# Low parts of a kernel's weights made by ScalarE and an accumulating DMA instead of by VectorE

## What is computed

```python
u = rmsnorm(h, norm_g[l])
proj = jnp.einsum('bld,de->ble', u, w_in[l])
hq, hf, hi, hz, aq, ak, av, az, ga, gb = jnp.split(proj, offs, axis=-1)
oA = hgrn2_chunked(...)          # gated linear recurrence, per head
oB = ...                         # softmax attention of two components, per head
yA = jnp.einsum('blw,wd->bld', oA * jax.nn.silu(hz), w_branch_a[l])
yB = jnp.einsum('blw,wd->bld', oB * jax.nn.silu(az), w_branch_b[l])
m = jax.nn.sigmoid(ga) * yA + jax.nn.sigmoid(gb) * yB
h = h + jnp.einsum('bld,de->ble', m, w_out[l])
out = rmsnorm(h, final_g)
```

## Time and profile before

| | |
|---|---|
| profiled execution | 753.44 us (span 751.7 us) |
| median of three runs | 753.66 us |
| TensorE busy | 731.2 us, 97% of the span |
| VectorE busy | 453.1 us, 60% |
| ScalarE busy | 281.0 us, 37% |
| GpSimd busy | 23.0 us, 3% |
| VectorE's low parts (line 252) | 104 x 1222 ns = 127.1 us |
| ScalarE's high parts (line 247) | 104 x 1052 ns = 109.4 us |
| DMA | 63.44 MB, 27.8% of 16 engines' span |

### The profile page before, as it was taken

The page is one execution under the profiler, slowest core; times in us unless marked ns, Lnnn a source line. Parts: engine busy times, 40 slices in busy tenths (PEclk is TensorE's granted clock), DMA queues, the critical chain, the costliest instruction groups (busy, mean ns, idle before and its releaser), DMA issues.

```text
span 751.7 us, 12966 instructions
## 1 busy us (share of the span) xinstructions
PE 731.2 (97%) x4665; PEld 653.9 (87%) x4665; DVE 453.1 (60%) x1019; ACT 281.0 (37%) x548; POOL 23.0 (3%) x34
## 2 busy tenths in 40 slices
PE   2999999999999999999999999999999999999996
PEld 2998999999899899999989989998888888888885
DVE  4567569568667856956866785695643333233342
ACT  5414442642552444264155235425423222232232
POOL 2000000000000000000000000000000000000000
PEclk9899999999999999999999999999999999999999
DMA  7421220230122132023012213302323323323603
GB/s 265 122 76 57 86 84 12 72 112 28 56 87 81 50 90 84 2 82 112 28 56 84 84 35 104 85 1 85 112 85 112 95 87 98 112 84 98 237 29 113
DMA packets 105416, 63.44 MB, mean 84 GB/s; under 512 B 2066, under 2 KB 100772, under 8 KB 105396
## 3 DMA queue, kind: packets, MB, share of 16 engines
q1 hardware_dynamic: 105076, 62.52, 27.5%
q10 hardware_dynamic: 320, 0.66, 0.3%
HBM read 61.07 MB, written 2.10 MB: 84 GB/s over the span
## 4 chain that ended last, share of the span: by engine, by line
PE 96%; SPq 1%; issue 1%; DMA 1%; DVE 0%; ACT 0%; POOLq 0%; POOL 0%; DVEq 0%; ACTq 0%
PE ps L385 26%; PE ps L386 26%; PE ps L387 26%; PE ps L506 3%; PE ps L576 2%; PE ps L602 2%; PE ps L492 1%; PE ps L593 1%; PE ps L603 1%; PE ps L540 1%; PE ps L539 1%; PE ps L547 1%; PE ps L522 1%; DMA rows_in<-in_da_norm_g 1%; PE ps L531 1%
## 5 line engine op out<-in xcount | busy, mean ns | idle before, releaser
L385 PE MATMUL ps<-uT_hi,w_hi 128*128 128x512 f32 (+3 forms) x960 | 321.6, 335 | 0.0
L386 PE MATMUL ps<-uT_lo,w_hi 128*128 128x512 f32 (+3 forms) x960 | 308.7, 322 | 0.0
L387 PE MATMUL ps<-uT_hi,w_lo 128*128 128x512 f32 (+3 forms) x960 | 307.9, 321 | 0.0
L385 PEld LDWEIGHTS ps<-uT_hi,w_hi 128*128 128x128 f32 x960 | 181.6, 189 | 16.4 <-issue 3.2
L252 DVE TENSOR_TENSOR w_lo<-w_raw,w_hi 128x1024 fp32r<-128x1024 f32 x104 | 127.1, 1222 | 109.9 <-ACT w_hi L247 108.9
L387 PEld LDWEIGHTS ps<-uT_hi,w_lo 128*128 128x128 f32 x960 | 181.1, 189 | 13.9
L386 PEld LDWEIGHTS ps<-uT_lo,w_hi 128*128 128x128 f32 x960 | 181.6, 189 | 11.6
L247 ACT ACTIVATE w_hi<-w_raw 128x1024 fp32r<-128x1024 f32 x104 | 109.4, 1052 | 87.5 <-PE ps L387 84.3
L808 ACT ACTIVATE e<-e,small 128x144 f32<-128x144 f32 (+3 forms) x64 | 36.1, 565 | 41.9 <-DVE small L1200 41.9
L375 POOL TENSOR_TENSOR small<-small 128x4 f32<-128x4 f32 x16 | 16.1, 1008 | 507.3 <-DVE small L1135 362.7
L1133 DVE TENSOR_REDUCE small<-sq 128x4 f32<-128x512 f32 x16 | 11.0, 686 | 33.3 <-ACT sq L800 33.3
(11 more groups left out here) (185 smaller groups left out, 993.4 us busy)
## 6 DMA issues: line engine op xcount, KB each, us to landing
w_raw<-in_w_in SPq DMA_DIRECT2D x80, 512.0 KB, 3.7
w_raw<-in_w_branch_a SPq DMA_DIRECT2D x8, 512.0 KB, 3.6
w_raw<-in_w_branch_b SPq DMA_DIRECT2D x8, 512.0 KB, 3.6
w_raw<-in_w_out SPq DMA_DIRECT2D x8, 512.0 KB, 3.8
x_in<-in_x SPq DMA_DIRECT2D x4, 512.0 KB, 7.8
x_res<-in_x SPq DMA_DIRECT2D x4, 512.0 KB, 6.4
out<-y_out SPq DMA_DIRECT2D x8, 256.0 KB, 2.3
rope<-in_c_rope SPq DMA_DIRECT2D x1, 528.0 KB, 6.0
```

Source lines behind the costliest of these rows:

```text
L385: pe.matmul(dst, w[0], rhs[0], start=start, stop=False, skip_group_check=True)
L386: pe.matmul(dst, w[0], rhs[1], start=False, stop=False, skip_group_check=True)
L387: return pe.matmul(dst, w[1], rhs[0], start=False, stop=stop, skip_group_check=True)
```

## The change

Units 0 to 6 stay as they were. From unit 7 on (`BY_DMA` = 7) VectorE makes no low parts. ScalarE writes, right behind the high part, its negative into `w_lo` (`scale=-1.0` on the raw unit), and a DMA that GpSimd issues adds the raw unit to it in place. Two semaphores `low_added` count these DMAs, for even and odd ones. SP waits for them in `low_seen`, ahead of the load that reuses the place in `w_raw`, and counts up `lo_ready` for TensorE. GpSimd's order puts the adds of `conv(0)` and `conv(1)` ahead of a head's first power, those of `conv(2)` to `conv(6)` between the two powers and that of `conv(7)` behind the second.

```diff
@@ convert_hi @@
         act.activation(w_hi[:, slot, :], w_raw[:, slot % RAW, :], ACT.Copy).then_inc(hi_ready, 1)
+        if not isinstance(u, int) or u >= BY_DMA:
+            act.activation(w_lo[:, slot, :], w_raw[:, slot % RAW, :], ACT.Copy, scale=-1.0).then_inc(neg_ready, 1)
+    def add_raw(pool, p, u, slot):
+        pool.wait_ge(neg_ready, u - BY_DMA + 1)
+        pool.sem_inc(adds_begun, 1)
+        pool.dma_start(w_lo[:, slot, :], w_raw[:, slot % RAW, :], accum_op=ALU.add).then_inc(low_added[p % 2], 16)
@@ sync @@
+            def low_seen(h, u):
+                if h is None and u < BY_DMA:
+                    sp.wait_ge(lo_ready, u + 1)
+                    return
+                done = 16 * ((u - BY_DMA) // 2 + 1)
+                sp.wait_ge(low_added[(u - BY_DMA) % 2], done if h is None else 64 * h + done)
+                sp.sem_inc(lo_ready, 1)
             def load(u, slot, src):
-                if not isinstance(u, int):
-                    sp.wait_ge(lo_ready, u - RAW + 1)
-                    sp.sem_inc(slot_free, 1)
-                elif u >= RAW:
-                    sp.wait_ge(lo_ready, u - RAW + 1)
+                if u[0] is not None or u[1] >= RAW:
+                    low_seen(u[0], u[1] - RAW)
...
                 load((None, O0 + 4 + c), c, w_out[:, 2 * c:2 * c + 2, 512:1024])
+            for u in (ALL_UNITS - 2, ALL_UNITS - 1):
+                low_seen(None, u)
@@ gpsimd @@
-            with pool.Fori(0, 2 * HEADS) as b:
-                pool.wait_ge(ms_ready, b + 1)
+            def rstd_pow(n):
+                pool.wait_ge(ms_ready, n)
                 pool.tensor_tensor(rstd[:, 0:CH], ms[:, 0:CH], half_neg[:, 0:CH], ALU.pow).then_inc(rstd_ready, 1)
+            def low(h, p):
+                add_raw(pool, p, SECTIONS * h + BY_DMA + p, (7 + p) % SLOTS)
+            with pool.Fori(0, HEADS) as h:
+                low(h, 0)
+                low(h, 1)
+                rstd_pow(2 * h + 1)
+                for p in range(2, 7):
+                    low(h, p)
+                rstd_pow(2 * h + 2)
+                low(h, 7)
+            with pool.Fori(0, KT // 2) as i:
+                for p in range(SECTIONS):
+                    low(i + HEADS, p)
+            add_raw(pool, 0, ALL_UNITS - 1, (ALL_UNITS - 1) % SLOTS)
@@ vector @@
-                conv(0)
...
-                conv(7)
-            for u in range(O0 + 3, ALL_UNITS):
-                convert_lo(dve, u, u % SLOTS)
```

More of the change, by code:

```diff
@@ L55 @@
 AHEAD = 4
+BY_DMA = 7
 T0 = SECTIONS * HEADS
@@ L215, in build @@
     slot_free = sem("slot_free")
+    adds_begun = sem("adds_begun")
+    neg_ready, low_added = sem("neg_ready"), [sem(f"low_added{i}") for i in range(2)]
     hi_ready, lo_ready, w_used = sem("hi_ready"), sem("lo_ready"), sem("w_used")
@@ L309, in _ @@
                 if i == 1:
-                    section(0, 0, 0, 0)
-            section(0, 1, 1, 1)
+                    section(0, 0, (None, 0), 0)
+            section(0, 1, (None, 1), 1)
             sp.dma_start(rows_in[0:2 * HEADS, :], lb_logits.rearrange("r (h p) -> (r h) p", p=P)) \
@@ L321, in _ @@
             sp.dma_start(bias[:, :], c_bias).then_inc(tables_in, 16)
-            section(0, 2, 2, 2)
-            section(0, 3, 3, 3)
-            with sp.Fori(0, HEADS - 1) as h:
+            section(0, 2, (None, 2), 2)
+            section(0, 3, (None, 3), 3)
+            for p in range(SECTIONS):
+                section(p // 4, (p + 4) % 8, (None, AHEAD + p), p % 4)
+            with sp.Fori(0, HEADS - 2) as i:
                 for p in range(SECTIONS):
-                    section(h if p < 4 else h + 1, (p + 4) % 8, SECTIONS * h + AHEAD + p, p % 4)
+                    section(i + 1 if p < 4 else i + 2, (p + 4) % 8, (i, SECTIONS + AHEAD + p), p % 4)
@@ L327, in _ @@
             for p in range(SECTIONS - AHEAD):
-                section(HEADS - 1, AHEAD + p, T0 - 4 + p, p)
+                section(HEADS - 1, AHEAD + p, (None, T0 - 4 + p), p)
             for d in range(2):
                 for j, col in enumerate((GA, GB)):
-                    load(T0 + 2 * d + j, 2 * d + j, w_in[:, :, col + d * P:col + (d + 1) * P])
+                    load((None, T0 + 2 * d + j), 2 * d + j, w_in[:, :, col + d * P:col + (d + 1) * P])
             for d in range(2):
                 for j, w in enumerate((w_branch_a, w_branch_b)):
-                    load(T0 + 4 + 2 * d + j, 2 * d + j, w[:, :, d * P:(d + 1) * P])
+                    load((None, T0 + 4 + 2 * d + j), 2 * d + j, w[:, :, d * P:(d + 1) * P])
@@ L335, in _ @@
             with sp.Fori(0, KT // 2 - 1) as i:
                 for dd in range(2):
-                    u = T0 + 8 + 8 * i + 4 * dd
+                    u = T0 + 8 + 4 * dd
                     at_d = i * (2 * P) + (2 + dd) * P
[L339 to L342, removed]
+                    load((i, u + 0), 0, w_in[:, :, bass.ds(at_d + GA, P)])
@@ L343, in _ @@
+                    load((i, u + 1), 1, w_in[:, :, bass.ds(at_d + GB, P)])
+                    load((i, u + 2), 2, w_branch_a[:, :, bass.ds(at_d, P)])
+                    load((i, u + 3), 3, w_branch_b[:, :, bass.ds(at_d, P)])
             for c in range(4):
-                load(O0 + c, c, w_out[:, 2 * c:2 * c + 2, 0:512])
+                load((None, O0 + c), c, w_out[:, 2 * c:2 * c + 2, 0:512])
             sp.wait_ge(w_used, O0 - 2)
@@ L351, in _ @@
             for c in range(4):
-                load(O0 + 4 + c, c, w_out[:, 2 * c:2 * c + 2, 512:1024])
+                load((None, O0 + 4 + c), c, w_out[:, 2 * c:2 * c + 2, 512:1024])
+            for u in (ALL_UNITS - 2, ALL_UNITS - 1):
+                low_seen(None, u)
             for i in range(CH):
@@ L1068, in chain @@
                     chained()
-                def conv(p):
-                    convert_lo(dve, SECTIONS * h + 7 + p, (7 + p) % SLOTS)
                 def gate(branch):
@@ L1246, in head @@
                 masked(1)
-                conv(1)
                 probs(0)
@@ L1261, in head @@
                 masked(2)
-                conv(2)
                 norm(0, B_HG)
-                conv(3)
                 probs(2)
                 gated(0)
-                conv(4)
                 gate(1)
@@ L1271, in head @@
                 probs(3)
-                conv(5)
-                conv(6)
                 norm(1, B_A)
-                conv(7)
                 gated(1)
@@ L1312, in _ @@
                 for dd in range(2):
-                    for j in range(4):
-                        at_u = T0 + 11 + 4 * dd + j
-                        convert_lo(dve, 8 * i + at_u, at_u % SLOTS)
                     dve.wait_ge(gate_taken, 4 * i + 2 * dd + 6)
```

4 lines of the change are left out of this document (removed).

## The result

The changed kernel takes 888.96 us (median of four runs, 888.31 to 891.97), the kernel before 753.22 us in the same sitting (752.64 to 753.78). The ratio is 1.1806 [1.179, 1.1822], 18% slower. The profiled execution's span is 890.2 us against 751.7.

What follows compares the result with a forecast made beforehand. TensorE was taken to bound the kernel, holding 96% of the chain that ended last. On 753.44 us, 85 in the heads and 7 at the end made 845, stated as 846 against the median; range 795 to 925.

Steps and rivals of the forecast that it cites:

- VectorE's relief: Whole kernel: the 118 us taken off VectorE ran beside TensorE, which waits for none of it; gain 0.
- the likeliest case: Case with 4.5 to 6.5 us from the negative's end until TensorE sees the unit: 820 to 887 us, chance 0.44.
- Step 1: In each head, conv(0)'s unit 8h+7: its low part comes 2.3 us late for TensorE.
- Step 2: In each head, conv(1)'s unit 8h+8: its low part comes 0.25 us late.
- Step 3: In each head, conv(2)'s unit 8h+9: its add stands behind the first power in GpSimd's queue, 5.35 us late.
- Step 4: In each head, conv(4)'s load waits for conv(2)'s add, delaying probs_out and TensorE's last scores by 0.5 us.
- Step 5: In each head, conv(5), conv(6): negatives and a late load delay the fourth block's probs_out by 2.25 us.
- The clock: Behind the 5.35 us stall: possibly 2.5 us more per head, left out; as rival 866 us, chance 0.1.
- After the heads: Units 71 to 103: w_raw places take 5.7 us per unit, 0.26 too slow; 8.6 us hidden by lead, 0 lost.
- The end: Projection's right half, first block: unit 103 at least 3.5 us late, 8.7 if places lag; 7 us taken.
- the slow add: Rival: over 6.5 us from the negative's end until TensorE sees the unit; 940 us at 7.8, chance 0.19.
- The fast add: Rival: under 4.5 us from the negative's end until TensorE sees the unit; 799 us at 3.7, chance 0.25.

Runs made afterwards that it cites:

- after: The changed kernel as profiled, with DMA adds from unit 7 on, against the kernel before: span 890.2 us against 751.7.
- the clock held up: Changed kernel plus 16 throwaway TensorE matmuls ahead of the wait for conv(2)'s unit, in seven of eight heads: 888.06 us, ratio 1.1785.
- ScalarE's copy alone: Kernel before, with ScalarE writing the negative and VectorE adding the raw unit, no DMA adds: 760.4 us, ratio 1.0087.
- the copy: Changed kernel with a plain DMA copy of the raw unit into w_lo in place of the add (low parts wrong): 818.91 us.
- half the columns: Changed kernel with each DMA adding only the first 512 of a unit's 1024 columns: 815.73 us.
- the tail alone: Kernel before, with DMA adds for units 71 to 103 only and VectorE making units 7 to 70: 793.47 us, ratio 1.0503.
- the last kernel: Kernel before, with DMA adds for units 71 to 101, four raw places from unit 72, VectorE making units 102 and 103: 752.95 us, ratio 0.9989.

## Why the prediction was right, and what it missed

The direction and the mechanism held: TensorE waits for late low parts, and VectorE's relief gives nothing. The time came out at 889.0 us, inside the range of 795 to 925, which is 130 us wide, but 43 us above the forecast and 2 above the likeliest case's own range. A, the time from the negative's end until TensorE sees the unit, was not the reason for that: the parts that the trace shows, 0.6 us from the negative's end to GpSimd's issue (403.72 to 404.29), 4.6 to the landing and some 0.1 for SP, make 5.3 us against the 5.5 assumed.

- **Step 1, conv(0), 2.3 us:** right, 1.81.
- **Step 2, conv(1), 0.25:** no wait seen; right in being nothing.
- **Step 3, conv(2) behind the power, 5.35:** the wait is right, 4.37, and shown by moving the add (0.88). But taking the order away gave back only 1.3 us per head. The prediction's own sign of being wrong was under 2 us for this step: as a wait it is far from it, as a price it falls under it, since the wait of step 4 stands behind it and grows. GpSimd, just done with the power, issues at once, and TensorE goes on 4.7 us later (392.22 to 396.91), not A = 5.5.
- **Step 4, the last scores, 0.5:** hidden in after (0.0), but mis-sized. It took the load behind the add at 3.7 us. In after it took 4.6 (397.06 to 401.69), with step 3's order taken away 6.6, beside the next add, and there this step costs 3.33 us; with the clock held up, 1.36.
- **Step 5, conv(6), 2.25:** right, 1.78; 0.56 of it is ScalarE's copy alone (0.65 in the working).
- **Missed in the head:** conv(7)'s load was taken as harmless, as its unit is wanted only in the next head. But ScalarE waits 4.49 us for it, `split_hi(1)` stands behind it in ScalarE's order, and at the next head's start TensorE waits 1.32 us for VectorE's `q` (line 531). The load was issued at 416.44 and took 6.3 us beside the add of 415.36. That VectorE was held up through ScalarE's order fits the order of the rows. The wait is absent with the copy and with half the columns, where the adds land sooner, but no run took it away alone. Seven of these make 8.8 us.
- **The head's sum:** 10.65 forecast, 12.6 measured. The four waits make 9.3; 1.6 is the slow stretch, the rest (1.7) is not settled; conv(0)'s waits of 3.49 us in the first head and 3.94 in the last are a part of it. That the sum came so near is partly luck: the forecast steps came out 2.7 us smaller (8.0), and 4.6 us came from what the working left out.
- **The clock:** leaving it out of the sum was right for the changed kernel, for the reason given: what it takes, the ring gives back. When the clock is kept, 1.36 us appear at the scores in place of the 1.6, so that these 1.6 us are a part of the head's account and not a price of their own. The rule of the Trainium skill (TensorE: Matmul & The Clock Gate, "Why this matters for your kernels") that a gap drops the clock agrees with the trace (0.50 after 4.9 us with 0.54 of work); keeping the clock up behind this wait did not change the time.
- **After the heads, 0 for the ring:** this is the term that failed most. The working had 11.4 us for a place's round, two units in it; measured are 12.2 in after, 13.3 with the tail alone. Its 5.7 us per unit was 0.26 above TensorE's pace and so hidden by the lead. At 6.1 to 6.65 it is not. Each transfer was sized as if alone. With the tail alone the add lands after 6.3 us, and in after the loads of `w_branch_a`, which run beside an add, land after 4.8. The formula itself was sound: with A = 7.0 (6.3 + 0.6 + 0.1) it gives 6.45 us per unit, 33 less 7 of lead, and with the 7 at the end an estimate of 33 us, where 35 to 40 were measured. Four places in the ring took 36.6 of 40 us away.
- **The end, 7 us:** too small: three waits of 13.9 us, and a mean clock of 0.84 over the last 60. The first of them, 5.61, is behind an add that took 9.4 us beside the loads of `x_res`. The working took `x_res` into its 7 without a price of its own.
- **VectorE's relief, 0:** right behind the heads, shown by the last kernel. In the heads it is argued, from rows that show TensorE waiting there for nothing before.

Term by term against 753.2 us: heads 85 forecast, 101 measured; after them 7 forecast, 40 measured alone and 35 as the rest of the whole.

Of the rivals, the slow add did not come (5.3, not above 6.5), though beside a load the add's 6.3 + 0.6 + 0.1 = 7.0 us is in its range after the heads. The fast add was priced too low as well: with a copy, A is 0.6 + 3.0 + 0.1 = 3.7, for which the prediction had 799 us, and the run gave 818.9. The same holds for the slope: 1.6 us of A were worth 70 us, 44 per us, where the working had 47 for 1.8, or 26 per us. By the first product with `oa_hi` (601.1 us with the copy) 50 us of this lie in the heads and 23 behind them, where the working gives 37 and 5 for 1.6 us of A. So about 18 of the missing us are behind the heads, where the working let the ring's cost begin only above A = 5.5. The other 13 are in the heads, where it left out the wait at `q` and that transfers take longer side by side; that these two make the 13 is not shown.

The Trainium skill's half rate (Collectives: The Full Stack, "The bandwidth ceiling") and its 3.2 us for a plain DMA (DMA: Bandwidth & Descriptors, "Anatomy of one DMA — SWDGE (gpsimd) path") gave an estimate of 4.4 and 3.2 us; the runs show 4.6 and 3.0. They agree within 0.2 us. The prediction's own figure, 4.4 us without GpSimd's part (3.7 + 0.7), came as near from rows of loads.

## What to carry to other kernels

A step whose latency goes up by a few us costs nothing while it has units of lead and nobody waits for its source; it is paid at the points where an in-order queue or a buffer's reuse takes the lead away. Before you move work to a DMA, list who waits for its source buffer as well as its result, and size each transfer with the others that will run beside it: the ring's round decides, not the single latency. A wait's length is not its price. When one wait is removed, expect the next to take over a large part of it: here 4.37 us at one place became 0.88 there and 3.33 at another, and 1.3 us per head were won.

## What the runs showed of the hardware

- An adding DMA of 512 KB from SBUF to SBUF lands 4.6 us after its issue, a copy of the same bytes 3.0, an add of 256 KB 3.3; over 97 units the add takes 32.0% of 890 us of the queues' time, the copy 18.0% of 817 us, about half.
- GpSimd's issue is 0.90 us for an add whatever its size, 0.54 for a copy.
- Where loads of 512 KB run beside it nearly all the time, the add lands after 6.3 us (median of 33) with two places and 5.6 to 5.7 with four. Beside the four loads of `x_res` two adds took 9.4 us each.
- Behind a wait of 4.37 us (after) and one of 2.74 us (with the copy) TensorE goes on at a granted clock of 0.50 for 2 us and about 0.7 for the next 2, which is 1.6 us of work less. In after, keeping the clock up gained nothing, as a later wait grew by 1.36 us.
- DMA engines at a busy share of 0.81 take nothing from TensorE (194.19 against 193.85 us in 200).
